# Feature-major projection chunks: three 256-column matmuls per weight tile in place of a 512- and a 256-column one, and two independent copies in place of a copy and an addition

## The reference

```python
proj = rms_norm(h, g) @ w_in                 # 2048 x 7832: sparse attention beside a recurrence
y = mix @ w_out;  h = h + rms_norm(y, post)  # 2048 x 2048
q, k, v, g = split(rms_norm(x) @ a_w_in, 4)  # 2048 x 8192: differential attention
x = x + (o * silu(g)) @ a_w_out
q, k, v, g, lr = split(rms_norm(x) @ b_w_in) # 2048 x 6160: gated linear attention
x = x + (o * silu(g)) @ b_w_out
```

## Time and profile before

| | us |
|---|---|
| median of 3 runs | 2080.61 |
| lowest, highest | 2070.24, 2082.86 |
| span of the profiled execution | 2085.6 |
| TensorE busy (matmuls) | 1798.1 |
| VectorE busy | 958.0 |
| ScalarE busy | 713.6 |

### The profile page before, as it was taken

How to read it: one execution, slowest core, us unless ns; L and a number is a source line. 1 busy time by engine, 2 the same in 40 slices (tenths; PEclk the granted TensorE clock), 3 DMA queues, 4 the chain that set the end, 5 groups by cost and what they waited for, 6 DMA issues and landing times. The chain is left out here.

```text
span 2085.6 us, 22741 instructions
## 1 busy us (share of the span) xinstructions
PE 1798.1 (86%) x9532; PEld 1525.2 (73%) x9532; DVE 958.0 (46%) x1036; ACT 713.6 (34%) x800; POOL 36.0 (2%) x33
## 2 busy tenths in 40 slices
PE   3899999945999997795899999987695999994588
PEld 2688888833998886684788888864484888883476
DVE  1444444446343333744544444439545444445644
ACT  1333433442110123533434334336334333334132
POOL 0000000014000000000000000000000000000000
PEclk9899999966776687998899999979798999997899
DMA  8755554630000003153456656350152555552053
GB/s 196 166 182 184 190 190 131 172 92 0 1 1 1 1 2 114 41 182 121 138 186 188 194 185 198 122 174 1 41 198 86 186 179 179 182 182 82 0 163 119
DMA packets 140588, 258.08 MB, mean 124 GB/s; under 512 B 4469, under 2 KB 28611, under 8 KB 139924
## 3 DMA queue, kind: packets, MB, share of 16 engines
q1 hardware_dynamic: 140500, 256.83, 39.4%
HBM read 250.00 MB, written 6.82 MB: 123 GB/s over the span
## 5 line engine op out<-in xcount | busy, mean ns | idle before, releaser
L333 PE MATMUL ps<-xt_in,in_wh 128*128 128x512 f32 x2224 | 790.6, 400 | 29.1 <-DVE in_wl L289 28.7
L289 DVE TENSOR_TENSOR in_wl<-w_raw,in_wh 128x2048 fp32r<-128x2048 f32 (+2 forms) x192 | 403.5, 2103 | 550.0 <-ACT in_wh L239 549.9
L334 PE MATMUL ps<-xt_in,in_wl 128*128 128x256 f32 x2224 | 628.2, 282 | 0.0
L239 ACT ACTIVATE in_wh<-w_raw 128x2048 fp32r<-128x2048 f32 (+2 forms) x192 | 338.7, 1766 | 620.2 <-PE ps L334 502.0
L333 PEld LDWEIGHTS ps<-xt_in,in_wh 128*128 128x128 f32 x2224 | 422.2, 190 | 132.2 <-DVE in_wl L289 27.8
L334 PEld LDWEIGHTS ps<-xt_in,in_wl 128*128 128x128 f32 x2224 | 425.5, 191 | 0.0
L340 PE MATMUL ps<-out_wh,xt_out 128*128 128x512 f32 x384 | 152.2, 396 | 34.1 <-DVE out_wl L289 34.1
L289 DVE TENSOR_TENSOR out_wl<-w_raw,out_wh 128x2048 fp32r<-128x2048 f32 x48 | 109.7, 2291 | 139.9 <-ACT out_wh L239 139.9
L341 PE MATMUL ps<-out_wl,xt_out 128*128 128x512 f32 x384 | 151.5, 395 | 0.0
L342 PE MATMUL ps<-out_wh,xt_out 128*128 128x512 f32 x384 | 151.1, 394 | 0.0
L239 ACT ACTIVATE out_wh<-w_raw 128x2048 fp32r<-128x2048 f32 x48 | 91.6, 1915 | 157.9 <-PE ps L342 157.9
(11 more groups left out here) (343 smaller groups left out, 1871.2 us busy)
## 6 DMA issues: line engine op xcount, KB each, us to landing
w_raw<-in_a_w_in SPq DMA_DIRECT2D x64, 1024.0 KB, 5.2
w_raw<-in_w_in SPq DMA_DIRECT2D x52, 1024.0 KB, 5.0
w_raw<-in_b_w_in SPq DMA_DIRECT2D x48, 1024.0 KB, 5.1
w_raw<-in_w_out SPq DMA_DIRECT2D x16, 1024.0 KB, 5.2
w_raw<-in_a_w_out SPq DMA_DIRECT2D x16, 1024.0 KB, 5.3
w_raw<-in_b_w_out SPq DMA_DIRECT2D x16, 1024.0 KB, 5.2
w_raw<-in_w_in SPq DMA_DIRECT2D x16, 512.0 KB, 3.7
bias_rows_dram<-proj SPq DMA_DIRECT2D x1, 3072.0 KB
```

The costliest lines, as they stand in the source:

```text
L239: nc.scalar.activation(wh[:, k4 % 2, :, 0:seg["width"]], k.raw[:, k4, :, 0:seg["width"]], ACT.Copy).then_inc(k.hi_made, 1)
L289: nc.vector.tensor_tensor(wl[:, k4 % 2, :, 0:seg["width"]], k.raw[:, k4, :, 0:seg["width"]], wh[:, k4 % 2, :, 0:seg["width"]].bitcast(F32) ...
L333: pe.matmul(o[:, 0:2 * S], h[:, cs], xt[:, kt, :], start=st, stop=False)
L334: last = pe.matmul(o[:, S:2 * S], l[:, cs], xt[:, kt, 0:S], start=False, stop=sp)
```

## The change

In a T segment the three products become three matmuls of 256 columns, all into columns 0 to 255 of the bank: high x high, high x low and low x high, summed by the accumulation. The sum is complete in PSUM, so the buffer `corr` and the addition go. A chunk is drained by two copies: ScalarE takes the first half of its tiles, VectorE the second, each when the last piece is done. A chunk of one tile is split by tokens instead, and there VectorE still waits for ScalarE, since both read one bank.

```diff
-        corr = sbuf(nc, ctx, f"{name}_corr", [P, 4, S])
...
                         nt = seg["width"] // P
-                        if not (isinstance(c, int) and c == 0):
-                            act.wait_ge(k.evac_b, c)
-                        nc.scalar.activation(corr[:, 0:nt, :], k.ps[:, 4 * par:4 * par + nt, S:2 * S],
+                        na, ta = (nt // 2, S) if nt > 1 else (1, P)
+                        nc.scalar.activation(seg["dst"](j)[:, 0:na, 0:ta], k.ps[:, 4 * par:4 * par + na, 0:ta],
                                              ACT.Copy).then_inc(k.evac_a, 1)
...
                         nt = seg["width"] // P
-                        dve.wait_ge(k.evac_a, c + 1)
-                        nc.vector.tensor_tensor(seg["dst"](j), k.ps[:, 4 * par:4 * par + nt, 0:S],
-                                                corr[:, 0:nt, :], ALU.add).then_inc(k.evac_b, 1)
+                        dve.wait_ge(k.piece_used, c * PIECES + PIECES)
+                        n0, t0 = (nt // 2, 0) if nt > 1 else (0, P)
+                        if nt == 1:
+                            dve.wait_ge(k.evac_a, c + 1)
+                        nc.vector.tensor_copy(seg["dst"](j)[:, n0:nt, t0:S],
+                                              k.ps[:, 4 * par + n0:4 * par + nt, t0:S]).then_inc(k.evac_b, 1)
...
                                     o = k.ps[:, 4 * par + ct, :]
                                     cs = slice(ct * P, ct * P + P)
-                                    pe.matmul(o[:, 0:2 * S], h[:, cs], xt[:, kt, :], start=st, stop=False)
-                                    last = pe.matmul(o[:, S:2 * S], l[:, cs], xt[:, kt, 0:S], start=False, stop=sp)
+                                    pe.matmul(o[:, 0:S], h[:, cs], xt[:, kt, 0:S], start=st, stop=False)
+                                    pe.matmul(o[:, 0:S], h[:, cs], xt[:, kt, S:2 * S], start=False, stop=False)
+                                    last = pe.matmul(o[:, 0:S], l[:, cs], xt[:, kt, 0:S], start=False, stop=sp)
```

## The result

The change makes the kernel slower by about one per cent: 2101.23 us, the median of four runs (2095.18 to 2108.79), against 2076.98 us, the median of four runs of the kernel before (2070.24 to 2082.86). The ratio is 1.0116, with a 95% interval of 1.0073 to 1.0159. The profiled execution took 2102.32 us with a span of 2100.3, so a time lies some 2 us above its span; the profile of before has a span of 2085.6, 14.7 us less. That profile is of a slow draw: its span alone is longer than the slowest of the four runs (2082.86), and its mean granted clock is 0.892, against 0.900 in the profile after.

A forecast was written before the change was run, and what follows sets the result against it. TensorE's matmul starts were taken to set the pace in the feature-major chunks. Added to the 2080.61 us median, +13.6 and +7.4 us for third matmuls and -0.7 us for drains gave 2101 us, range 2086 to 2112.

The forecast's parts named there:

- The bound: Feature-major chunks: TensorE sets the pace, so the change's price is what it does to the distance between matmul starts.
- The price of a matmul: Feature-major triples: 120 ns per 256-column matmul, 360 ns for three, as in token-major chunks; +21.0 us at full clock.
- the short pair: Feature-major 512- plus 256-column matmuls at 346.7 ns; 1022 pairs, each 13.3 ns dearer as a triple, 13.6 us.
- the long pair: Feature-major 512- plus 256-column matmuls at 353.3 ns; 1105 pairs, each 6.7 ns dearer as a triple, 7.4 us.
- The long pace: Feature-major stretches at 353.3 ns a pair: the unexplained 6.7 ns was expected to vanish, leaving triples at 360 ns.
- rival A: Feature-major chunks: the extra 6.7 ns stays, triples there take 366.7 ns; 2108 us, chance 0.17.
- Shared weights: Feature-major triples: the two high-part products share a stationary operand, yet each was expected to load its own weights.
- the rule of the skill: TensorE weight loads overlap running matmuls only across differing row groups; exposed third loads would add 234 us; forecast disagreed.
- rival C: Feature-major triples: the second high-part product finds its weights in place, a triple takes 347 ns; 2073 us, chance 0.06.
- rival B: Feature-major triples: small matmuls cost 117 ns each, a triple 351 ns; 2082 us, chance 0.08.
- Rival D: Feature-major chunks: the 360 ns pace isn't sustained, matmuls take 125 ns each; 2133 us, chance 0.05.
- The drains: One-tile chunks after full ones in in1 and in3: VectorE's shorter copy closes TensorE's gap; -0.7 us, between 0 and -1.6.

The follow-up runs named there:

- the grouped order: Kernel before the change, with each k-tile's four 512-column products issued first, then its four of 256; 2084.84 us over ten runs, ratio 1.0035.
- the reordered triple: Changed kernel with its products ordered high x high, low x high, high x low; 2102.7 us over ten runs, ratio 1.0078 to the kernel before.

## Why the prediction was right

**The bound.** Right: the feature-major chunks followed TensorE's starts, but for its few waits at a stage's start and at the one-tile chunks. The new drain by itself moved no time that can be measured.

**The price of a matmul.** Right, and the step that carried the forecast. The 256-column token-major triples said 120 ns each, and the changed chunks run at 120 in every stretch. The forecast for TensorE at full clock was +21.0 us less 0.7 for the drains; the three feature-major parts grew by 20.5. By stage: in1 858 x 6.7 ns = 5.7, measured 6.2; in2 756 x 13.3 = 10.1, measured 10.8; in3 3.5 + 1.7 = 5.2, measured 3.5. What is left over is drains, a wait and the clock. In in3 the waits at the one-tile chunks were 0.7 us shorter, and after the last of them TensorE worked at the lower clock for 6 us before and for 3.6 after, so that the mean clock of the 19.4 us from there was 0.85 before and 0.91 after. In in2 it is the reverse: the first 10 us had a mean clock of 0.83 before and 0.76 after. In in1 TensorE resumed after its wait for late weights at 93.52 us in place of 92.88. One step of the working is right only in its sum: the short pair was read as two matmuls of columns plus 13.3 ns, 226.7 and 120. By the mean distances between starts it is 230.1 for the wide and 116.6 for the narrow one, and the long pair 236.2 and 117.1. The price of the triple rested on the 256-column triples, and those hold.

**The long pace.** I took 360 ns in both paces and kept 366.7 as rival A's. Rival A fell: no stretch of the changed kernel shows it. The reason I gave, the mixing of widths, is supported by the kernels with one width only, which have one pace, but the grouped order shows that it isn't a charge per border, as I had made it in that experiment.

**Shared weights and the rule of the skill.** Line 335 loads its own weights, and the order of the products makes no difference: rival C fell. The Trainium skill, "TensorE: Matmul & The Clock Gate", section "The mechanism", would by the sentence that I took from it have exposed a load for each matmul; all triples show the load beside the matmul before it, as in the earlier trace rows. The same section of the Trainium skill also lets a load that targets the background weight buffer go ahead of running matmuls, and the triples, 120 ns apart with a load each, agree with that. The 2.5 ns over the columns that the same page of the Trainium skill gives are not what this kernel shows: 13.3 ns at 256 and at 512 columns in streams of one width. That also disposes of rival B: its premise was true, 117 ns for the narrow matmul of a pair, but it doesn't carry over to three in a row. Rival D (a pace that isn't sustained) fell with 638 steps of 360 ns.

**The drains.** Right in sign, too small: TensorE's idle time at the one-tile chunks of in1 and in3 went from 0.37 + 1.17 and 0.38 + 3.07 us to 0.79 and 2.72, 1.5 us less where I had put 0.7, though inside the range of 0 to 1.6. The gap of the earlier trace rows is closed: in the first one-tile chunk the copy (L299) is done in time and TensorE doesn't wait for what follows it, while the kernel with the matmuls alone still waits there. VectorE after the change, and TensorE with the old drain:

```profile
373.58 0.68 DVE L299 COPY proj<-ps 128x512 f32<-128x512 f32 x1
374.41 0.69 DVE L287 TENSOR_TENSOR in_wl<-w_raw,in_wh 128x512 fp32r<-128x512 f32 x1
```

```profile
375.54 0.39 PE L333 MATMUL ps<-xt_in,in_wh 128*128 128x256 f32 x1 [0.34 <-DVE in_wl L289]
```

**The point of reference.** The measured median, 2101.23 us, meets the forecast of 2101 more closely than the argument deserves. The sum was 20.3 us on a base of 2080.61; with the fourth run the base became 2076.98, and the difference of medians is 24.3 us, of the profiles 14.7. All three lie within what single executions differ by: ten runs of the unchanged kernel went from 2064.29 to 2093.11. The ratio of the kernel with three products over the most runs, that of the reordered triple, is +0.8% with an interval of 0.4 to 1.1. So the mechanism and its 20 us are shown in the traces; that the change lies beyond 1% rather than just under it is not settled by the runs.

## What to carry to other kernels

Price a matmul by the distance between starts, not by its duration or by busy time, and look for a place in the same kernel where the shape that you plan already runs: here 64 triples told the new pace to the nanosecond. A narrow matmul added in place of width cost 7 to 13 ns each time in this kernel, with every weight load hidden, so let TensorE stream its widest when it is the bound. Work taken from engines that wait for the bound (34 us here) is worth only what it does at the few places where they are late.

## What the runs showed of the hardware

- Float32r matmuls of one width, back to back at full clock, took their columns at 2.4 GHz plus 13.3 ns, at 256 columns (120 ns) and at 512 (226.7 ns). With two 128-column matmuls in every four, the weight loads took over: 120 ns from a load beside a wide matmul to the next, 112 beside a narrow one.
- With 512- and 256-column matmuls alternating, a pair took 346.7 or 353.3 ns, most of the difference on the wide one (230.1 and 236.2 ns). A value held while TensorE went on without a stop, and it changed only across a stop, twice without any fall of the granted clock; the same program drew one value in one execution and the other in the next. In fixed groups of four it took 351 ns throughout its profile. Why the two values exist stays open.
- Ten runs of the unchanged kernel spread over 28.8 us and ten with the new drain over 27.8, against 16.2 for the grouped order and 14.0 for the reordered triple. The two paces may have a part in that (some 2100 pairs at 6.7 ns are 14 us), but the time goes with the granted clock, which can account for the spread without them: the unchanged kernel's lowest run had a mean clock of 0.903 and its highest 0.892, the new drain's 0.904 and 0.892; the reordered triple's had 0.903 and 0.896, the grouped order's 0.900 and 0.893.
- The first layer's mixers, untouched, took 6.0 us less in the changed kernel's profile, at a mean clock of 0.75 against 0.73. An execution's draw of the clock can hide a third of what one looks for here, and only the comparison stage by stage keeps them apart.
